# The samples' attention as a fourth stage of the block, its keys and values streamed in rings, with 12 chunks of the input projection beside it

## What is computed

```
xn = rms_norm(x, norm_in)
u = jnp.einsum('btd,dc->btc', xn, w_in)                 # 2048 -> 12,000 columns
o_a = rwkv7_mixer(u_a ...)                               # 16 heads, a scan over tokens
o_b = nsa_mixer(q, gates, cmp_kv, sel_kv, win_kv ...)    # 16 query heads, 4 kv heads
merged = gate_a * (o_a @ w_pa) + gate_b * (o_b @ w_pb)
h = x + merged @ w_o
```

```
o_cmp, p_cmp = compressed_attention(q, cmp_kv ...)       # 127 pooled blocks
top_i = select_blocks(p_cmp ...)                         # 16 of 33 blocks of 64 tokens
o_sel = selected_attention(q, sel_kv, top_i ...)
o_win = window_attention(q, win_kv ...)                  # the last 512 tokens
o = g[0] * o_cmp + g[1] * o_sel + g[2] * o_win
```

## Time and profile before

| | |
|---|---|
| median of 3 runs | 2623.42 us (2622.43 to 2625.33) |
| profiled execution, its own time | 2622.69 us |
| its span, first to last instruction | 2620.5 us |
| mean granted TensorE clock | 0.946 |
| PE busy | 88% of the span |
| DVE, ACT, POOL busy | 45%, 30%, 17% |
| moved by DMA | 301.65 MB, mean 115 GB/s |

### The profile page before, as it was taken

The page is one execution under the profiler, slowest core; times in us unless marked ns, Lnnn a source line. Parts: engine busy times, 40 slices in busy tenths (PEclk is TensorE's granted clock), DMA queues, the critical chain, the costliest instruction groups (busy, mean ns, idle before and its releaser), DMA issues. The chain is left out here.

```text
span 2620.5 us, 51046 instructions
## 1 busy us (share of the span) xinstructions
PE 2308.7 (88%) x21174; PEld 2102.2 (80%) x21174; DVE 1187.0 (45%) x2330; ACT 790.7 (30%) x1494; POOL 441.7 (17%) x239
## 2 busy tenths in 40 slices
PE   5999999999999999999999789999246637999996
PEld 4998989898988888899999777888223327999996
DVE  4244545444454545348898144444223425443223
ACT  4343333333332332122222344544111113232111
POOL 0000000000000000001100499999200000000000
PEclk8999999999999999999999899999668877999998
DMA  3321222222221212268775513221575632342232
GB/s 116 98 83 60 83 64 75 64 79 60 80 79 60 80 62 85 75 198 287 226 254 186 153 57 93 69 85 44 164 236 170 189 115 103 124 146 106 102 101 93
DMA packets 124556, 301.65 MB, mean 115 GB/s; under 512 B 24218, under 2 KB 37156, under 8 KB 118596
## 3 DMA queue, kind: packets, MB, share of 16 engines
q1 hardware_dynamic: 97972, 242.44, 29.1%
q0 software_dynamic: 7696, 32.78, 3.6%
q10 hardware_dynamic: 18688, 23.59, 2.8%
HBM read 261.55 MB, written 45.54 MB: 117 GB/s over the span
## 5 line engine op out<-in xcount | busy, mean ns | idle before, releaser
L177 PE MATMUL acc<-xh,w_hi 128*128 128x272 f32 x3008 | 670.5, 304 | 24.0 <-DVE xl L433 12.0
L177 PE MATMUL acc<-xh,w_lo 128*128 128x272 f32 x3008 | 624.8, 289 | 0.0
L177 PE MATMUL acc<-xl,w_hi 128*128 128x272 f32 x3008 | 623.8, 289 | 0.0
L177 PEld LDWEIGHTS acc<-xh,w_hi 128*128 128x128 f32 x3008 | 472.1, 190 | 76.0 <-issue 45.4
L177 PEld LDWEIGHTS acc<-xl,w_hi 128*128 128x128 f32 x3008 | 475.7, 190 | 0.0
L177 PEld LDWEIGHTS acc<-xh,w_lo 128*128 128x128 f32 x3008 | 473.4, 190 | 0.0
L160 DVE TENSOR_TENSOR w_lo<-w_raw,w_hi 128x1024 fp32r<-128x1024 f32 x166 | 203.2, 1224 | 412.6 <-ACT w_hi L152 411.5
L152 ACT ACTIVATE w_hi<-w_raw 128x1024 fp32r<-128x1024 f32 x188 | 198.5, 1056 | 301.1 <-PE acc L177 245.7
L1171 DVE SCALAR_TENSOR_TENSOR b_C<-b_rows,b_pos_s,b_C 128x512 f32<-128x512 f32 x240 | 162.4, 743 | 0.0
L893 PE MATMUL rbank<-m 64*64 64x64 f32 x3840 | 130.9, 220 | 1.1 <-DVE m L584 1.1
L893 PEld LDWEIGHTS rbank<-m 64*64 64x64 f32 x3840 | 118.8, 135 | 15.2 <-issue 3.8
(11 more groups left out here) (386 smaller groups left out, 3350.6 us busy)
## 6 DMA issues: line engine op xcount, KB each, us to landing
w_raw<-in_w_all SPq DMA_DIRECT2D x188, 512.0 KB, 3.6
b_rows<-in_cmp_rows SPq DMA_DIRECT2D x128, 256.0 KB, 3.7
d_kv<-in_sel_kv SPq DMA_DIRECT2D x128, 256.0 KB, 2.9
m_w<-in_w_mo SPq DMA_DIRECT2D x32, 1024.0 KB, 5.7
m_gates<-tmp_uT SPq DMA_DIRECT2D x16, 544.0 KB, 3.7
out_s_win<-in_win_in POOLq DMA_DIRECT2D x8, 1016.0 KB, 5.8
tmp_uT<-ub POOLq DMA_DIRECT2D x24, 272.0 KB, 2.3
tmp_uT<-ub ACTq DMA_DIRECT2D x23, 272.0 KB, 2.6
```

The lines of the kernel that those rows point to most:

```text
L177: ins = self.nc.tensor.matmul(acc[:, c, 0:HALF], w[:, k % KH, :], x[:, k, c * HALF:(c + 1) * HALF], start=(k == 0 and m == 0), stop=(k == ...
```

## The change

- `attend_samples` becomes a fourth stage of the one block. The 94 chunks are shared out anew: 41, 25, 16 and 12 (were 57, 25, 12 and none). The order of the chunks changes with it: the pairs' chunks first, then the queries', then keys and values, then the rest.
- In `rwkv` a pair has (41 * 8 - 72) / 8 = 32 pieces in place of 48; the gaps of `PAIR_JOBS` stay as weights, and a job's place is their running sum times 32, divided by 48. DVE now signals the mixing of every field, not of four together.
- In the new stage each of the 84 jobs has a place; 24 pieces go ahead of PE's `enter`, the other 72 are spread evenly over the jobs. Some jobs of the next pair of samples (small scores, importance chain) lie among those of the present one.
- Keys and values are two input arrays now, so a page's keys are 128 KB and its values 128 KB. Both go through rings of three units; a unit is the window or four pages of both samples of the pair (1 MB). SP loads key units, POOL value units; unit u + 3 is loaded when PE has done the job that reads unit u. The samples' numbers are known when the program is built, so each page has its own `value_load` and DMA.
- The score and value matmuls all have 32 columns of weights; a value matmul has 128 moving columns. Selected weights are kept in tiles, exponents are taken tile by tile. Sums and minima come out of fused instructions.
- Blocks are opened with `no_gpsimd_drain=True`, and there is one barrier fewer.

```diff
-FRONT_CHUNKS, KEY_CHUNKS = 57, 82
+FRONT_CHUNKS, KEY_CHUNKS, PROMPT_CHUNKS = 41, 66, 82
 def chunk_order():
-    plain = list(range(33, 49)) + list(range(62, 70))
-    order = [LORA_CHUNK] + PAIR_CHUNKS(0) + PAIR_CHUNKS(1)
...
+    pairs = [c for p in range(8) for c in PAIR_CHUNKS(p)]
+    others = [c for c in range(33, N_CHUNK) if c not in Q_CHUNKS and c not in KV_CHUNKS]
+    return [LORA_CHUNK] + pairs + list(Q_CHUNKS) + KV_CHUNKS + others
 def job_tables():
-    place, pair = {}, sum(j[4] for j in PAIR_JOBS)
+    place, gaps = {}, sum(j[4] for j in PAIR_JOBS)
+    pair = (FRONT_CHUNKS * PIECES - FIRST_PIECES) // 8
...
-            place[i, name] = FIRST_PIECES + pair * i + at * span // pair
+            place[i, name] = FIRST_PIECES + pair * i + at * span // gaps
...
-PROMPT_PIECES, START_PIECES = PIECES * (N_CHUNK - KEY_CHUNKS), 16
+PROMPT_PIECES, START_PIECES = PIECES * (PROMPT_CHUNKS - KEY_CHUNKS), 16
...
+N_BP, N_UNIT, N_RING = DEC_B // 2, 5, 3
+SAMPLE_PIECES, SAMPLE_START = PIECES * (N_CHUNK - PROMPT_CHUNKS), 24
+def sample_jobs():
+    order = [(name, 0) for name in ("sm", "ptc", "imp", "imp2")]
+    for bp in range(N_BP):
+        for name in ("W", "K0", "sm+", "K1", "K2", "K3", "ptc+", "TW", "imp+", "Tn", "T0", "PW", "imp2+", "T1", "P0",
+                     "T2", "P1", "T3", "P2", "P3", "Pn"):
+            if name[-1] != "+":
+                order.append((name, bp))
+            elif bp + 1 < N_BP:
+                order.append((name[:-1], bp + 1))
...
+        place[job] = SAMPLE_START + (k + 1) * (SAMPLE_PIECES - SAMPLE_START) // len(order)
...
+        def load_unit(eng, u, ring, landed, window, pages):
+            bp, n = divmod(u, N_UNIT)
+            for b2 in range(2):
+                b = 2 * bp + b2
+                dst = ring[u % N_RING][:, b2, :, :]
+                if n == 0:
+                    eng.dma_start(*window(dst, b)).then_inc(landed[u % N_RING], 16)
+                    continue
+                for p in range(4):
+                    at = b * N_PAGES + 4 * (n - 1) + p
+                    page = eng.value_load(table[0:1, at:at + 1], min_val=0, max_val=N_POOL - 1)
+                    eng.dma_start(dst[:, p, :], A[pages][bass.ds(page, 1)].rearrange("a p n -> (a p) n"))\
+                        .then_inc(landed[u % N_RING], 16)
 # on SP:
+            for job in order:
+                background(place[job])
+                if job[0] == "sm" and job[1] + 1 < N_BP:
+                    sp.wait_ge(pe_jobs, done_at[job])
+                    load_kc(job[1] + 1)
+                if job in KEYS and KEYS.index(job) + N_RING < len(KEYS):
+                    sp.wait_ge(pe_jobs, done_at[job])
+                    load_keys(KEYS.index(job) + N_RING)
 # on POOL:
+            for u, job in enumerate(VALUES):
+                if u + N_RING < len(VALUES):
+                    pool.wait_ge(pe_jobs, done_at[job])
+                    load_unit(pool, u + N_RING, vU, v_in, window, "sel_v")
+                if job[0] == "P3" and job[1] + 1 < N_BP:
+                    pool.wait_ge(pe_jobs, done_at["Pn", job[1]])
+                    load_vcn(job[1] + 1)
 # on PE:
+            def values(b, bp, n):
+                u = N_UNIT * bp + n
+                taken(pe, (("TW", "T0", "T1", "T2", "T3")[n], bp))
+                pe.wait_ge(v_in[u % N_RING], arrivals(u))
+                c0 = P if n == 0 else 0
+                for c in range(4):
+                    for b2, gp in PAIRS:
+                        ins = mm(b[rows(b2, gp), c0:c0 + P], PT[u % 3][:, c, rows(b2, gp)],
+                                 vU[u % N_RING][:, b2, c, gp * P:(gp + 1) * P], start=(n <= 1 and c == 0), stop=False)
...
+            background(SAMPLE_START)
+            enter(pe)
...
-            for stage in (rwkv, rest, attend_prompt):
+            for stage in (rwkv, rest, attend_prompt, attend_samples):
```

More of the change, by code:

```diff
@@ L115, in end, with enter @@
         eng.sem_inc(self.stage_ended, 1)
[L117 removed]
+    def enter(self, eng):
         eng.wait_ge(self.stage_ended, 4 * self.n_ended)
[L120 to L121 removed]
+        eng.wait_ge(*self.pe_end)
 class Projection:
@@ L1578, in _ @@
                 lows[0] += 1
+            T.end(pool, W.w_lo, W.h_ahead)
         @block.scalar
@@ new lines, in attend_samples, with taken @@
+        stored = [sem(f"d_stored{j}") for j in range(2)]
+        N_CONSTS, N_Q = 5, 9
+        enter = T.enter
+        def taken(eng, *jobs):
+            for e, sem_ in (("act", ev_act), ("dve", ev_dve)):
+                counts = [out_at[j][1] for j in jobs if j is not None and out_at[j][0] == e]
+                if counts:
+                    eng.wait_ge(sem_, max(counts))
+        KEYS = [(name, bp) for bp in range(N_BP) for name in ("W", "K0", "K1", "K2", "K3")]
+        VALUES = [(name, bp) for bp in range(N_BP) for name in ("PW", "P0", "P1", "P2", "P3")]
@@ new lines, in attend_samples @@
+        arrivals = lambda u: 16 * sum(2 if m % N_UNIT == 0 else 8 for m in range(u % N_RING, u + 1, N_RING))
+        def load_unit(eng, u, ring, landed, window, pages):
[11 more added lines that the diff above has]
+                        .then_inc(landed[u % N_RING], 16)
@@ L1958, in _ @@
+            background(SAMPLE_PIECES)
+            store(N_BP - 1)
+            act.wait_ge(sent, 16 * N_BP)
+            for j in range(2):
+                act.wait_ge(stored[j], 16 * ((W.s1 - W.s0 + 1 - j) // 2))
+            T.end(act, None, 0)
         @block.vector
@@ new lines, in _, with background, got, lowest @@
+            link = same_engine(dve, chain)
+            lows = [W.h0 + 2]
+            def background(upto):
+                while lows[0] < W.h_ahead and HALF_PIECES * (lows[0] - W.h0 - 2) <= upto:
+                    W.low(dve, lows[0])
+                    lows[0] += 1
+            def got(job):
+                background(place[job])
+                dve.wait_ge(pe_jobs, done_at[job])
+                return bank[:, bank_of[job], :]
+            def lowest(out, a, b, into):
+                return ttr(out=out, in0=a, in1=b, scale=-1.0, scalar=3e38, op0=ALU.add, op1=ALU.min, accum_out=into)
```

663 lines of the change are left out of this document (379 added, 284 removed).

## The result

The changed kernel takes 2646.24 us (median of four runs, 2642.76 to 2650.40) against 2622.93 for the kernel before in the same comparison. The ratio is 1.009 with a 95% interval of 1.0074 to 1.0105: slower by 0.9%. The forecast was 2601, faster; 2646 lies inside its wide range, on the other side of "before". The profiled execution took 2650.4 us, 4 above its median, with a span of 2648.3.

A forecast was written before the change was run, and what follows sets the result against it. PE was taken as the bound (busy 88%, no room in the scan), with 144 idle us in the samples' stage. -95 + 36 + 38 - 1 = -22 from 2623.4 gave near 2601 us, range 2535 to 2672.

The forecast's parts named there:

- Piece and change of shape: PE's prices: 1.505 us for one piece, 0.19 us for leaving and coming back to jobs of another shape.
- The scan's stalls: `rwkv`, per pair: O waits behind U, 0.56 us in plain chunks, 2.6 or 3.1 where `w_lo` falls; 13.7 us.
- -95: `rwkv`, in us: seven pairs 11.6 shorter each (81), the last one 14; bounds -193 and about -24.
- The prompt: Prompt's stage: 32 more pieces are 48.2 us, 12 of it filling PE's idle time; +36, bounds +23 and +55.
- The side remark on POOL: Prompt's stage: about ten more `w_lo` add 24 us to POOL's 347, making 371, under PE's 390 or so.
- The samples' stage: Sum over PE's order, 322.5 us, +38: pieces 144.5, attention 95, shape changes 12, the rest start, waits and clock.
- Start: Samples' stage: its start costs 7 us, bounds 0 and 20.
- Keys: Samples' stage: PE waits at K3 for key pages, 9.6 us a pair, 38 in all, bounds 0 and 50.
- Values: Samples' stage: PE waits at P3 for value pages, 1.31 us each on POOL; 3.0 a pair, 12 in all.
- A: Samples' stage: pages land before PE asks, so ring waits and most of the clock's 6 us go; 2545 us; chance 0.20.
- B: Samples' stage: value pages on POOL are dear, deciding from 1.68 us a page; 2655 us at 2.2; chance 0.25.
- C: The scan doesn't stall: `rwkv` gives nearly the whole 193 us, kernel about 2505 us; chance 0.09.

The follow-up runs named there:

- x9: x1 with the scan's gaps one piece on each side of U, x7's places, and POOL's prompt `w_lo` later except the first; 2490.9 us, ratio 0.9497.
- x3: Changed kernel plus three matmuls that compute nothing behind U's matmul in every second scan chunk; 2619.3 us, ratio 0.9987.
- x1: Changed kernel with DVE making a due `w_lo` in the scan behind the state's update, not ahead of UV or the update; 2556.4 us, ratio 0.9746.
- x4: Changed kernel with DVE making all the prompt's `w_lo` ahead of each of its jobs, POOL none; 2733.0 us, ratio 1.0418.
- x8: Changed kernel with chunks shared out as before (57, 25, 12, none) in the old order, no pieces in the samples' stage; 2610.5 us, ratio 0.9956.
- x6: x1 with four pages of a sample loaded by one transfer from fixed places, without `value_load`; 2485.9 us, ratio 0.9472.
- x7: x1 with the 18 pieces of a pair of samples placed by hand, mostly ahead of K3 and P3; 2518.7 us, ratio 0.9597.
- x11: x1 with DVE making all the prompt's `w_lo`, only at the end of a unit's work; 2616.6 us, ratio 0.9971.

## Why the prediction was wrong

**Piece and change of shape**: right. 16 pieces fewer take 25.2 us off a pair's busy time at full clock (117.2 before, 92.0 in x9), where the forecast took off 24.1, and the change of shape is 0.20 in the samples' stage.

**The scan's stalls**: right, and by the mechanism that the forecast named. 13.7 us of waits for UV and 1.8 in the matrices' chain were forecast, 13.2 and 1.8 are in the trace. The lower bound of 24 us for the scan, however, doesn't follow from its own terms: stalls of 3.5 in eight chunks, less the 3 of now, are 25 us a pair and more than the 24.1 that the pieces give, so the scan would have given nothing.

**What failed in the scan** is the step from there to the time. The sum put every matmul at the duration of a row at full clock, though the forecast itself created waits of 2.6 to 3.1 us and the samples' windows of before showed what gaps do to the clock (0.74). The clock was a term in the samples' stage and missing in the scan. x3 shows the cause. Over the six pairs between the first and the seventh mark of L969, PE's busy time is 28.8 us above what the forecast's pieces leave (587.7 against 558.9, at a clock of 0.94), and its idle time 7 below the forecast, which makes 22 us. The last pair is 4.8 short of its 14, and its busy time alone is 7.4 above that of x1, whose clock there is 1.00 (0.90 here). The first pair gave 5.1 in place of 11.6, which wasn't split. Together these are the 33 us by which -95 was off.

**The prompt**: +36 forecast, +33 measured, and by the mechanism named: 47.4 us more of busy time (48.2 forecast) and 14.5 less idle (12). The idle time that was filled isn't that at the start, though, which is still 12.8. The side remark on POOL was wrong, and cost more than the stage's own error: POOL's work was to stay under PE's 390. The work did grow by the 24 us of the forecast, but it stands in one order with waits for ACT's `w_hi`. These grew from 0.8 to 32.9 us, which made the steps 419 us long. The forecast added busy times where the order of two engines counted.

**The samples' stage**: +38 forecast, +60 measured. PE's idle time is 98.4 us, where the terms for start, keys, values and short waits add up to 65; its busy time is 245.1, 12 less than the other terms.
- Start: 7 us forecast, 30 measured (18.0, then 4.5 and 0.9 more for `w_lo`, 5.9 for DVE's row and 1.1), above its bound of 20. POOL's late end is the cause of most of it (x4: 20 us off the stage with POOL early).
- Keys: 38 and 39.3.
- Values: 12 and 26.5, although a page on POOL cost 1.15 and not 1.31. By the numbers the reason is the cover: a value job was to take 2.6 us and takes 1.08 (0.034 a pass, below the lower bound of 0.06). Three such jobs ahead of P3 are 4.6 us a pair less cover. A matmul ahead of a ring's wait can't save time by being cheap; it only turns into wait. The forecast's terms for jobs and for waits were not independent. x8 shows the like in the large: with no pieces, PE's busy time in the stage is 37 us less than before (102.3 against 139.7), and the stage only 13 us shorter.
- Short waits on ACT and DVE: 8 forecast, 2.2 measured behind the start.
- Clock: expected near 1, measured 0.85.

**The rivals.** A (2545) comes near to what x6 makes of the stage (274.8; A gives some 266), but nothing made it so here. B had the right sign and nearly the right time (2655), by a mechanism that did not occur: its condition was a page price above 1.68 us. C was refuted by the pair of 112.8.

The stages' difference is +27.8 where -22 was forecast. Of these 50 us, 33 are the scan (its clock, of which the slightly smaller stalls gave a little back), 22 the samples' stage (the start alone was 23 too low), and -3 and -2 the prompt and `rest`. The 0.85 of the samples' stage is little the start's: from 1852 to the stage's end the clock is 0.86. x6 gives 19 us of busy time to the rings; where the rest of the low clock comes from isn't shown.

## What to carry to other kernels

Work taken out from between the jobs of a dependency chain gives back its time only as far as it wasn't the chain's cover: 193 us out of the scan gave 62. Before filling an idle stage elsewhere, look at what each engine does first when a job's result comes: here one matter of order (preparing weights for later ahead of the result that PE waits for) was worth 90 us, four times what the change lost. Where a ring's loads are issued one by one, cover has to stand in the windows in which a unit is under way (x7, 36 us of stage), and evenly spread filler misses them.

## What the runs showed of the hardware

- TensorE's waits of 2.5 to 3.1 us in a stretch that is otherwise full: in the pair shown three of four were followed by some 3 to 7 us at the lower clock level (pairs of projection matmuls 0.66 against 0.41 us), the first was not. Filling 2.15 us of each with matmuls that compute nothing brought a pair from 0.94 to 0.98 and made the kernel 27 us faster.
- A subtraction of two SBUF tensors on VectorE went from 1.22 us to 3.56 on average beside GpSimd's long instructions (x11), and each one that met them ended 1.1 to 1.2 us after the end of one of them; the stage went from 388 to 460 us, all of it while GpSimd was at work. GpSimd's own instruction was held up too, 9.74 us in the row shown against 8.95.
- Passes of 128 columns with 32 columns of weights, for four column groups in turn, take 0.034 us each at full clock (32 in 1.08), half of what 24 passes of the small scores had shown.
- A page of 128 KB by `value_load` and DMA takes 1.15 us to issue on GpSimd and 1.13 on SyncE in runs of 16, and lands after 3.0 and 2.8 us: no difference that matters.
